# Turning the whole U tiles in an earlier layer, into a DRAM table, and issuing all whole tiles of the expert stage from SP

## The chip, the cores and the metric

The kernel runs on one core of one Trainium2 chip. The metric is the device time of one execution in microseconds (us); 3 executions of the kernel before are shown.

## The reference, cut to what matters

Two transformer blocks follow each other on one sequence of 256 tokens with D = 2048, all in float32. The first is gated linear attention and a SwiGLU feed-forward layer, the second has three attention forms and then a layer of retrieved experts:

```
def swiglu(h, w_gu, w_down):                       # first block; 2 x 5632 columns, then 5632 -> 2048
    g, u = jnp.split(h @ w_gu, 2, axis=-1)
    return (jax.nn.silu(g) * u) @ w_down

def peer_ffn(hn, w_pq, sub_keys, u_tab, v_tab):    # last layer: 16384 experts, 8 heads x top 16 per token
    ...
    expert = ia * PEER_N_KEYS + ib
    gate = jax.nn.softmax(best_s, axis=-1)
    def token_block(args):                         # two blocks of 128 tokens
        a = jnp.einsum('td,ted->te', xb, u_tab[eb])
        hidden = gb.astype(xb.dtype) * jax.nn.gelu(a)
        return jnp.einsum('te,ted->td', hidden, v_tab[eb])
```

Every token thus needs 128 rows of `u_tab` and 128 rows of `v_tab`, each 8 KB, named by indices that are known only once the keys have been scored.

## The kernel before, in words

**Streamed part.** 292 weight tiles of 1 MB pass in order through a ring of 4 slots (`ring`), loaded from SP's queue (L594 is that loop). ACT writes the leading part of each half tile ("unit") to `WH` (L512, or L514 and L515), DVE the rest to `WL` (L527, or L531), and TensorE multiplies leading and rest parts (L633). `WH` and `WL` hold 4 units, so the splitting is at most 4 units ahead of TensorE. The feed-forward layer is 22 chunks of 4 tiles (`gu_chunk`) and then 44 tiles of `w_down`; DVE's part of the latter is a loop of 4 rounds of 8 tiles. POOL has no work there; its next step is the bias load at L1377, after `down_added`.

**Expert stage.** When the last streamed tile is split, the memory of the ring, of `WH`, `WL` and of the operands becomes 12 slots of one row tile each (128 x 2048 floats, 1 MB). `ROW_ORDER` is a fixed list of row tiles that all engines walk in order; row tile `n` uses slot `n % 12`, and is loaded only once row tile `n - 12` has been read. It has four kinds:
- `u`, 256 of them, in 16 groups of 16 (a group is one head of one token block): one expert row per token, gathered by POOL (L1405) and multiplied and summed on DVE (L2566). After a group, its 16 `hidden` values per token are made from these sums.
- `v`, 256 of them: gathered by POOL. Some go to TensorE, as a product with a diagonal matrix that ACT makes from `hidden` (L1873, then L1313), the others to DVE (L2570). `LEADS` says how many v tiles are put among the u tiles of each group, all of these for TensorE; the rest follow after group 15, where about one in eight is TensorE's.
- `turned`, 32 of them: whole tiles of 128 consecutive rows of `u_tab`, loaded by POOL (L1400). These 4096 experts are computed for all tokens, and the gathers leave their rows out. TensorE turns a tile in four parts (L1249), ACT copies each part from PSUM to SBUF (L1895), and TensorE multiplies it with the turned activations (L1260). The last two parts are handled only when the walk reaches the next v or turned tile (`finish_u`). `U_TILES` says how many stand in each group.
- `dense`, 32 of them: the whole tiles of `v_tab` that belong to them, loaded by POOL (L1400), multiplied by TensorE (L1300), all after group 15.

POOL issues every load of this stage in the order of the list, each behind a wait for its slot:

```
                elif n >= ROWS:
                    by, count = ROW_DONE[n - ROWS]
                    pool.wait_ge(sem({"dve": "rows_dve", "pe": "rows_pe", "turned": "raw_turned"}[by]), count)
```

## Time and profile before

| | |
|---|---|
| time, median of 3 executions | 3148.67 us (3145.7 to 3165.38) |
| the profiled execution: its own time, its span | 3147.76 us, 3146.0 us |
| busy in the span: TensorE, DVE, ACT, POOL | 2904.2, 2150.8, 1225.1, 974.6 us |
| expert stage, from POOL's first gather to the end | 1801.9 to 3146.0 us |
| bytes moved by DMA | 793.69 MB, of them 475.94 MB from POOL's queue and 313.73 MB from SP's |

"Busy" of TensorE contains modelled ends of pipelined matmuls. The share of time in which the 16 DMA engines were busy, and the bytes per second that they moved, stand by stretch in the rows below. A wait for several semaphores is put down to the one that came last.

### The profile page before, as it was taken

How to read it: one execution, taken by the hardware profiler on the slowest of the kernel's cores; microseconds unless marked ns; L12 is line 12 of the kernel's file. 1: busy time of each engine (PE TensorE's matmuls, PEld its weight loads, DVE VectorE, ACT ScalarE, POOL GpSimd, SP SyncE). 2: the span in 40 equal slices, each digit the busy share in tenths (PEclk: the TensorE clock that was granted, in tenths of full speed). 3: DMA queues.
4: the chain of work that ended last, by engine and by line, in shares of the span. 5: the costliest groups of instructions: out<-in, count | busy, mean ns of one | idle time of the engine just before them, and what ended most of it. 6: DMA issues, size and time to landing. Idle time of an engine off the chain costs nothing.

```text
span 3146.0 us, 38089 instructions
## 1 busy us (share of the span) xinstructions
PE 2904.2 (92%) x13724; PEld 2187.2 (70%) x13724; DVE 2150.8 (68%) x2908; ACT 1225.1 (39%) x2125; POOL 974.6 (31%) x599
## 2 busy tenths in 40 slices
PE   9999999999999999999999949888888989978987
PEld 8888788888888889998888945554555655533333
DVE  5686665555565545465565887888887668887777
ACT  5555555555553345355655521111111235700000
POOL 0011000000000000000000056777764678886774
PEclk9999999999999999999999979999998999999998
DMA  7444545555555555543443468999997899999997
GB/s 272 146 165 145 185 182 190 188 187 187 188 185 187 187 187 181 189 157 137 153 177 143 182 262 322 366 380 377 370 365 294 321 338 366 360 389 389 387 405 300
DMA packets 128209, 793.69 MB, mean 252 GB/s; under 512 B 30982, under 2 KB 30998, under 8 KB 32670
## 3 DMA queue, kind: packets, MB, share of 16 engines
q0 software_dynamic: 84000, 475.94, 39.2%
q1 hardware_dynamic: 43920, 313.73, 27.4%
q8 instruction: 90, 1.47, 0.2%
q10 hardware_dynamic: 144, 2.10, 0.2%
q14 instruction: 55, 0.45, 0.0%
HBM read 925.55 MB, written 4.22 MB: 296 GB/s over the span
## 4 chain that ended last, share of the span: by engine, by line
PE 69%; POOL 9%; DVE 8%; DMA 8%; issue 3%; ACT 3%; DVEq 0%; ACTq 0%; SPq 0%; POOLq 0%
PE ps L633 48%; POOL rows L1405 9%; PE ps L1313 6%; PE ps L1260 4%; DMA rows<-peer_v 4%; DMA rows<-peer_v,arena 3%; PE ps L1300 3%; DVE arena L2566 3%; PE ps L1249 1%; PE ps L741 1%; DVE WL L531 1%; ACT arena L1885 0%; PE ps L941 0%; PE ps L1291 0%; DMA rows<-peer_u,arena 0%
## 5 line engine op out<-in xcount | busy, mean ns | idle before, releaser
L531 DVE SCALAR_TENSOR_TENSOR WL<-ring,PA,WH 128x512 fp32r<-128x512 f32 x896 | 633.2, 753 | 459.5 <-ACT WH L515 442.6
L1313 PE MATMUL ps<-rows,rstd 128*128 128x512 f32 x1108 | 531.9, 632 | 158.1 <-ACT rstd L1873 103.4
L2566 DVE CUSTOM_DVE_ANT_0 arena<-rows,arena 128x2048 f32<-128x2048 f32 x256 | 586.9, 2292 | 64.5 <-DMA rows<-peer_u,arena 25.8
L514 ACT ACTIVATE WH<-ring,PA 128x512 fp32r<-128x512 f32 x448 | 324.1, 723 | 545.8 <-PE ps L633 398.4
L1405 POOL DMA_INDIRECT rows<-peer_u,arena x256 | 456.2, 1782 | 213.5 <-DVE WL L531 85.1
L1313 PEld LDWEIGHTS ps<-rows,rstd 128*128 128x128 f32 x1108 | 217.8, 202 | 428.6 <-issue 366.6
L1405 POOL DMA_INDIRECT rows<-peer_v,arena x256 | 447.0, 1746 | 171.5 <-issue 65.5
L633 PE MATMUL ps<-WH,HH 128*128 128x512 f32 x1120 | 442.3, 395 | 4.2 <-DVE WL L531 4.2
L633 PE MATMUL ps<-WH,HL 128*128 128x512 f32 x1120 | 437.7, 391 | 0.0
L633 PE MATMUL ps<-WL,HH 128*128 128x512 f32 x1120 | 437.2, 390 | 0.0
L2570 DVE SCALAR_TENSOR_TENSOR XR<-rows,arena,XR 128x2048 f32<-128x2048 f32 (+1 forms) x119 | 276.7, 2325 | 79.9 <-DMA rows<-peer_v,arena 71.3
L515 ACT ACTIVATE WH<-ring,PA 128x512 fp32r<-128x512 f32 x448 | 317.1, 708 | 0.0
L633 PE MATMUL ps<-HH,WH 128*128 128x256 f32 x1088 | 309.5, 284 | 4.7 <-DVE WL L531 3.2
L633 PE MATMUL ps<-HL,WH 128*128 128x256 f32 x1088 | 307.8, 283 | 0.0
L633 PE MATMUL ps<-HH,WL 128*128 128x256 f32 x1088 | 307.8, 283 | 0.0
L1377 POOL DMA_DIRECT2D arena<-bias_rows x2 | 1.8, 908 | 904.0 <-DVE XR L2275 904.0
L1300 PE MATMUL ps<-rows,arena 128*128 128x512 f32 x512 | 236.8, 618 | 37.7 <-DMA rows<-peer_v 37.7
L527 DVE TENSOR_TENSOR WL<-ring,WH 128x1024 fp32r<-128x1024 f32 x128 | 156.0, 1224 | 164.5 <-ACT WH L512 163.8
L633 PEld LDWEIGHTS ps<-WH,HH 128*128 128x128 f32 x1120 | 211.2, 189 | 49.1 <-DVE WL L531 5.7
L633 PEld LDWEIGHTS ps<-WH,HL 128*128 128x128 f32 x1120 | 210.8, 188 | 44.5
L633 PEld LDWEIGHTS ps<-WL,HH 128*128 128x128 f32 x1120 | 211.3, 189 | 43.1 <-issue 0.5
L1300 PEld LDWEIGHTS ps<-rows,arena 128*128 128x128 f32 x512 | 99.7, 198 | 173.0 <-issue 119.2
(391 smaller groups left out, 4186.6 us busy)
## 6 DMA issues: line engine op xcount, KB each, us to landing
ring<-stream SPq DMA_DIRECT2D x292, 1024.0 KB, 4.8
rows<-peer_u POOLq DMA_DIRECT2D x32, 1024.0 KB
rows<-peer_v POOLq DMA_DIRECT2D x32, 1024.0 KB
rows<-peer_u,arena POOLq DMA_INDIRECT x256
rows<-peer_v,arena POOLq DMA_INDIRECT x256
arena<-xT SPq DMA_DIRECT2D x4, 512.0 KB, 8.8
bias_rows<-bias_scratch POOLq DMA_DIRECT2D x1, 2048.0 KB, 11.4
arena<-xT ACTq DMA_DIRECT2D x1, 2048.0 KB, 10.7
```

The lines of the kernel that those rows point to most:

```text
L514: nc.scalar.activation(half_tile(WH, u)[:, 0:CH], raw_half(u)[:, 0:CH], ACT.Copy, scale=gain[0])
L515: nc.scalar.activation(half_tile(WH, u)[:, CH:UNIT], raw_half(u)[:, CH:UNIT], ACT.Copy, scale=gain[1]).then_inc(hi_done, 1)
L527: nc.vector.tensor_tensor(half_tile(WL, u), raw_half(u), half_tile(WH, u).bitcast(f32), ALU.subtract).then_inc(split, 1)
L531: ins = nc.vector.scalar_tensor_tensor(out=half_tile(WL, u)[:, s], in0=raw_half(u)[:, s], scalar=gain[d], in1=half_tile(WH, u).bitcast(f32 ...
L633: last = mm(o, l, r, start=start and n == 0, stop=stop and n == 2)
L741: last = mm(o, k[:, 2 * h + d, tk * P:(tk + 1) * P], q[:, 2 * h + d, tq * P:(tq + 1) * P], start=d == 0, stop=d == 1)
L1260: last = mm(ps[:, 4 + d // 2 % 2, d % 2 * TOK:(d % 2 + 1) * TOK], UT[q % 2][:, k, :], HNT[kt // 8][:, kt % 8, :], start=kt == 0, stop=kt = ...
L1300: last = mm(ps[:, 4 * tt + q, :], DENSE[c][:, tt * P:(tt + 1) * P], rows[:, SLOTS[n % ROWS], q * CH:(q + 1) * CH], start=False, stop=tt == ...
L1313: last = mm(ps[:, 4 * tt + q, :], DIAG[:, k % DIAGS, :], rows[:, SLOTS[n % ROWS], q * CH:(q + 1) * CH], start=n == mine[0], stop=n == ends[q])
L1405: nc.gpsimd.indirect_dma_start(out=rows[:, SLOTS[n % ROWS], :], out_offset=None, in_=u_tab if tab == "u" else v_tab, in_offset=bass.Indire ...
L2566: ins = V.tensor_tensor_reduce(out=JUNK, in0=rows[:, SLOTS[n % ROWS], :], in1=HN[:, tt, :], scale=1.0, scalar=0.0, op0=ALU.mult, op1=ALU.a ...
L2570: ins = V.scalar_tensor_tensor(out=XN[:, tt, s], in0=rows[:, SLOTS[n % ROWS], s], scalar=GA[:, tt, at:at + 1], in1=XN[:, tt, s], op0=ALU.m ...
```

## The change

- The feed-forward layer gets the turning of the 32 U tiles. POOL loads a tile of `u_tab` in four DMAs of 32 rows into two half buffers, in pieces of 512 floats. DVE turns each half with one `transpose` instruction, which turns blocks of 32 x 32 (`turn_tile`, two instructions per tile). POOL stores the 1 MB result to the new DRAM table `u_turned`, waits until it has landed, and loads the next tile. Tiles 0 to 19 are turned in the chunks 1 to 20 of the first matrix, one in each, between its 4th and 5th unit; the other 12 in the `w_down` loop, three in each round of 8 tiles, behind units 1, 6 and 11 of its 16.
- In the expert stage the turned tiles come from `u_turned`, and TensorE multiplies them directly (`turned_rows`). The transposes, ACT's copies and their buffers `UT` are gone. The activations are turned with a stride of 16 elements to match.
- SP issues the 64 whole tiles, POOL only the 512 gathers. Each whole tile still waits for its slot (`slot_free`); the dense ones wait on SP until all 16 groups' `hidden` are made.
- `LEADS` is 8 instead of 5 in groups 8 to 11 and 8 instead of 9 in groups 12 to 14, so 128 instead of 119 v tiles stand among the u tiles, and 128 instead of 137 behind them.

```
-LEADS = [0] + [9] * 7 + [5] * 4 + [9] * 4
+LEADS = [0] + [9] * 7 + [8] * 7 + [9]
 U_TILES = [2] * 8 + [4] * 4 + [0] * 4
...
+        U_TURNED, a = take(a, KD, 4, 32)
+        U_HALF0, _ = take(a, 2, 512)
+        U_HALF = [U_HALF0, rstd[:, :, :].rearrange("p (b x) t -> p b (x t)", b=2)]
+        u_turned = nc.dram_tensor("u_turned", (N_DENSE, P, D), f32, kind="Internal").ap()
...
+            def whole_rows(n, tile):
+                name, landed = ROW_IN[n]
+                slot_free(sp, n)
+                sp.wait_ge(sem(name), landed - 16)
+                sp.dma_start(rows[:, SLOTS[n % ROWS], :], tile).then_inc(sem(name), 16)
...
+            sp.wait_ge(sem("row_in2"), LANDED[2])
+            for n, (tab, d, _) in enumerate(ROW_ORDER):
+                if tab == "turned":
+                    whole_rows(n, u_turned[d])
             sp.wait_ge(sem("hidden"), GROUPS)
             sp.dma_start(GROW, bass.AP(gfin_row.tensor, 0, [[0, P], [1, D]])).then_inc(sem("gfin_in"), 16)
+            for n, (tab, c, _) in enumerate(ROW_ORDER):
+                if tab == "dense":
+                    whole_rows(n, v_tab[c * PEER_KEYS:(c + 1) * PEER_KEYS, :])
...
+            def turned_rows(n, d):
+                pe.wait_ge(sem(ROW_IN[n][0]), ROW_IN[n][1])
+                if d == 0:
+                    pe.wait_ge(sem("norm_leading"), 8 * len(TURNED) + 8)
+                if d % 2 == 0 and d >= 4:
+                    pe.wait_ge(sem("gelu_done"), 1 + d // 2 - 1)
+                u = rows[:, SLOTS[n % ROWS], :].rearrange("p (k i) -> p k i", i=P)
+                for k in range(KD):
+                    last = mm(ps[:, 4 + d // 2 % 2, d % 2 * TOK:(d % 2 + 1) * TOK], u[:, k, :], HNT[k // 8][:, k % 8, :],
+                              start=k == 0, stop=k == KD - 1)
+                last.then_inc(sem("rows_pe"), 1)
...
         @block.gpsimd
...
+            pool.wait_ge(sem("small_weights"), 4)
+            for d in range(N_DENSE + 1):
+                if d:
+                    pool.wait_ge(sem("small_weights"), 4 + 2 * d)
+                    pool.dma_start(u_turned[d - 1], U_TURNED.rearrange("p k b i -> p (k b i)")).then_inc(sem("row_in2"), 16)
+                    pool.wait_ge(sem("row_in2"), 16 * d)
+                if d < N_DENSE:
+                    for b in range(4):
+                        at = (U_ORDER[d] * PEER_KEYS + 32 * b) * D
+                        pool.dma_start(U_HALF[b // 2][:, b % 2, :], bass.AP(u_tab.tensor, at, [[512, 4], [D, 32], [1, 512]])).then_inc(sem(f"row_in{b // 2}"), 16)
...
         @block.vector
...
+            def turn_tile(d, i=0, per=0):
+                for h in range(2):
+                    dve.wait_ge(sem(f"row_in{h}"), i * (32 * per) + 32 * (d + 1))
+                    V.transpose(U_TURNED[:, :, 2 * h:2 * h + 2, :],
+                                U_HALF[h].rearrange("p b (d k) -> p k b d", k=KD)).then_inc(sem("small_weights"), 1)
...
                 for m in range(first, 8):
                     split_lo(dve, 2 * (T_GU + 4 * n) + UNITS + m, i)
+                    if 1 <= n < N_GU - 1 and m == 3:
+                        turn_tile(n - 1, i, 2)
...
+                    for m in range(8):
+                        split_lo(dve, 2 * (T_DOWN + 4 * j) + UNITS + m, i)
+                        if (j, m) in ((0, 1), (0, 6), (1, 3)):
+                            turn_tile(N_GU - 2 + 2 * j + m // 6, i, 3)
```

## Rows read from the trace of the kernel before

**Rows 1.** Page, 40 slices: busy share of the DMA engines in tenths.

```profile
DMA  7444545555555555543443468999997899999997
```

**Rows 2.** Stretches of the expert stage: length, busy and count by engine, clock, DMA share, GB/s.

```profile
core 0: us, PE busy (x) PEld busy (x) DVE busy (x) ACT busy (x) POOL busy (x), PEclk, DMA share, GB/s
1893.00:1967.00 74.00, 66.45 (x224) 39.20 (x223) 57.08 (x115) 11.90 (x30) 54.38 (x35) 0.95 0.91 347
1967.00:2318.00 351.00, 305.88 (x1021) 179.99 (x1020) 305.16 (x547) 53.72 (x135) 273.99 (x160) 0.96 0.97 375
2318.00:2567.50 249.50, 211.32 (x898) 150.60 (x896) 178.72 (x246) 51.54 (x109) 152.43 (x99) 0.96 0.84 315
2567.50:2741.00 173.50, 154.71 (x669) 94.39 (x667) 147.36 (x177) 108.40 (x285) 142.43 (x81) 0.95 0.96 363
2741.00:3134.00 393.00, 339.57 (x803) 149.53 (x802) 309.15 (x159) 21.85 (x50) 275.47 (x177) 0.95 0.96 383
```

**Rows 3.** The same view, two stretches of 8 us late in group 0.

```profile
1880.00:1888.00 8.00, 2.15 (x3) 1.15 (x4) 6.98 (x15) 0.62 (x2) 0.00 (x0) 0.50 0.02 10
1888.00:1896.00 8.00, 8.00 (x31) 5.22 (x31) 6.83 (x6) 0.60 (x1) 0.00 (x0) 0.85 0.00 0
```

**Rows 4.** Timeline, same time: start, duration, instruction, [idle before, releaser].

```profile
1885.85 5.91 PE L1313 MATMUL ps<-rows,rstd 128*128 128x512 f32 x8 [33.28 <-ACT rstd L1873]
...
1896.36 0.99 POOL L1405 DMA_INDIRECT rows<-peer_v,arena  x1 [19.46 <-PE ps L1249]
```

**Rows 5.** Waits, 2318 to 2567: who waited for whom, total us, times, longest.

```profile
POOL rows L1400 <- PE ps L1249: 47.0, 6, 15.7
POOL rows L1405 <- PE ps L1249: 32.4, 10, 6.2
```

**Rows 6.** Timeline of TensorE through one v tile and one turned tile, group 10.

```profile
2378.83 3.67 PE L1313 MATMUL ps<-rows,rstd 128*128 128x512 f32 x8 [1.17 <-ACT rstd L1873]
...
2382.34 1.89 PE L1260 MATMUL ps<-arena,UT 128*128 128x256 f32 x8
...
2384.07 0.60 PE L1249 MATMUL ps<-CO,rows 128*128 128x128 f32 x4
...
2390.13 1.04 PE L1249 MATMUL ps<-CO,rows 128*128 128x128 f32 x8
```

**Rows 7.** Groups of instructions: out<-in, count | busy us, mean ns.

```profile
L1400 POOL DMA_DIRECT2D rows<-peer_u x32 | 18.8, 588 | 57.3 <-PE ps L1249 57.2
```

**Rows 8.** Waits, 2741 to 3134.

```profile
DVE XR L2570 <- DMA rows<-peer_v,arena: 71.3, 39, 4.6
```

**Rows 9.** Stretches of the feed-forward layer: first matrix, then w_down.

```profile
360.00:920.00 560.00, 560.00 (x2535) 462.66 (x2534) 328.38 (x490) 303.55 (x493) 0.00 (x0) 1.00 0.51 186
...
938.00:1182.00 244.00, 243.61 (x1044) 196.19 (x1044) 124.40 (x113) 96.47 (x102) 0.00 (x0) 1.00 0.51 184
```

**Rows 10.** Chain that ended last: start, us; two chunks of the first matrix.

```profile
627.50 21.82 PE ps L633 x96
649.76 21.79 PE ps L633 x96
```

**Rows 11.** Groups of instructions, 938 to 1182: DVE and ACT per unit.

```profile
L527 DVE TENSOR_TENSOR WL<-ring,WH 128x1024 fp32r<-128x1024 f32 x84 | 102.9, 1225 | 117.6 <-ACT WH L512 117.6
...
L2252 DVE TENSOR_SCALAR A_h<-arena 128x1024 fp32r (+1 forms) x9 | 6.2, 689 | 0.0
...
L512 ACT ACTIVATE WH<-ring 128x1024 fp32r<-128x1024 f32 x84 | 89.1, 1061 | 143.2 <-PE ps L633 143.0 <-issue 0.3
```

**Rows 12.** DMA issues: KB each, median us from issue to landing.

```profile
ring<-stream SPq DMA_DIRECT2D x292, 1024.0 KB, 4.8
...
arena<-memT POOLq DMA_DIRECT2D x1, 2048.0 KB, 9.0
arena<-bias_rows POOLq DMA_DIRECT2D x1, 1024.0 KB, 6.9
...
arena<-bias_rows POOLq DMA_DIRECT2D x1, 512.0 KB, 4.9
```

More of the change, by code:

```diff
@@ L94 @@
 ROW_DONE = []
-RAW_TURNED = 24
-_count = {"dve": 0, "pe": 0, "turned": RAW_TURNED}
+_count = {"dve": 0, "pe": 0}
 for _tab, _g, _j in ROW_ORDER:
-    _by = "turned" if _tab == "turned" else "pe" if _tab == "dense" or _tab == "v" and by_matmul(PEER_K * _g + _j - N_LEAD) else "dve"
-    _count[_by] += 4 if _by == "turned" else 1
+    _by = "pe" if _tab in ("dense", "turned") or _tab == "v" and by_matmul(PEER_K * _g + _j - N_LEAD) else "dve"
+    _count[_by] += 1
     ROW_DONE.append((_by, _count[_by]))
-FINISHED_AT = {}
-for _n, (_tab, _g, _j) in enumerate(ROW_ORDER):
-    if _tab == "turned":
-        FINISHED_AT[_g] = next(n for n in range(_n + 1, ROW_LAST) if ROW_ORDER[n][0] in ("v", "turned"))
-SQUARE_AT, POLY_AT, TANH_AT, GELU_AT = ({FINISHED_AT[2 * p + 1] + later: p for p in range(N_DENSE // 2)} for later in (2, 5, 8, 11))
+SQUARE_AT, POLY_AT, TANH_AT, GELU_AT = ({ROW_AT["turned", 2 * p + 1, 0] + later: p for p in range(N_DENSE // 2)} for later in (4, 7, 10, 13))
 BATCH_AT = {}
@@ L118 @@
 FIRST_SHARED = N_ROWS - SHARED
+ROW_IN = []
+_landed = {f"weight_tile_in_slot{_s}": 16 * STREAMED // RING for _s in range(RING)}
+_landed.update({f"row_in{_s}": count for _s, count in enumerate(LANDED)})
+_tiles = 0
+for _n, (_tab, _g, _j) in enumerate(ROW_ORDER):
+    _name = f"row_in{_n % ROWS}"
+    if _tab in ("dense", "turned"):
+        _name, _tiles = f"weight_tile_in_slot{_tiles % RING}", _tiles + 1
+    _landed[_name] += 16
+    ROW_IN.append((_name, _landed[_name]))
 assert LAST_DENSE == N_ROWS - TAIL - 1
@@ L571, in hybrid_block, with slot_free @@
         IN2_AT = [T_IN2 + 4 * n for n in range(5)] + [T_SB + 4 * n for n in range(6)]
+        def slot_free(eng, n):
+            if n < 4:
+                eng.wait_ge(split, 2 * (N_TILES - 3 + n))
+            elif n < ROWS:
+                eng.wait_ge(used, 2 * (N_TILES - (2 if n < 6 else 1 if n < 8 else 0)))
+            else:
+                by, count = ROW_DONE[n - ROWS]
+                eng.wait_ge(sem(f"rows_{by}"), count)
         block = ctx.enter_context(nc.Block())
@@ L1252, in u_products @@
-            def u_products(d, part):
-                q = 4 * d + part
-                if d % 2 == 0 and part == 0 and d >= 4:
-                    pe.wait_ge(sem("gelu_done"), 1 + d // 2 - 1)
-                pe.wait_ge(sem("transposes_kept"), TT + q + 1)
-                for k in range(4):
-                    kt = 4 * part + k
-                    last = mm(ps[:, 4 + d // 2 % 2, d % 2 * TOK:(d % 2 + 1) * TOK], UT[q % 2][:, k, :], HNT[kt // 8][:, kt % 8, :],
-                              start=kt == 0, stop=kt == KD - 1)
-                last.then_inc(used, 1)
@@ L1386, in _ @@
             for n, (tab, g, j) in enumerate(ROW_ORDER):
[L1387 to L1397 removed]
                 if tab in ("dense", "turned"):
[L1399 to L1400 removed]
                     continue
+                slot_free(pool, n)
                 if tab == "u" and j == 0:
@@ L1881, in one_hots @@
                 else:
-                    act.wait_ge(used, 2 * N_TILES + 4 * N_DENSE)
+                    act.wait_ge(sem("rows_pe"), ROW_DONE[ROW_AT["turned", N_DENSE - 1, 0]][1])
                 v = ONE_HOT[n % 2]
@@ L1901, in square_u @@
             def square_u(p):
-                act.wait_ge(used, 2 * N_TILES + 8 * p + 8)
+                act.wait_ge(sem("rows_pe"), ROW_DONE[ROW_AT["turned", 2 * p + 1, 0]][1])
                 if U_ORDER[2 * p] // 8 in (2, 3):
@@ L1942, in _ @@
                     k += 1
-                    if turned is not None:
-                        keep_turned_u(turned, 2)
-                        keep_turned_u(turned, 3)
-                        turned = None
                 if tab == "u" and j == PEER_K - 1:
```

81 lines of the change are left out of this document (14 added, 67 removed).

## The prediction

> **What bounds the kernel now.** I first read the 40 slices of the page. The DMA engines are about half busy up to 1800 us, and 90% or more busy in most of what follows, except in one dip in the middle [rows 1]. So there are two kernels here. In the first TensorE sets the pace: in the feed-forward layer it is busy for 560.00 of 560 us and 243.61 of 244 us, with the DMA engines at 0.51 [rows 9]. The second is the expert stage. I then cut that stage at the first u tile of each group and asked for the busy shares. Groups 2 to 7 (1967 to 2318) have a DMA share of 0.97 at 375 GB/s while TensorE and DVE are each at 0.87; groups 12 to 15 and the v tiles after them are at 0.96 [rows 2]. To check that this is bytes: a gather leaves out a quarter of its rows, so it should move 0.786 MB, and a whole tile 1.049 MB. Six groups of 25 gathers and 2 whole tiles are 130 MB, and 130 MB in 351 us is 372 GB/s, which is the row. After group 15 it is also DVE that waits for data, 71.3 us in all [rows 8].
>
> Where the DMA engines aren't full, TensorE holds a slot. Groups 8 to 11 run at 0.84 and 315 GB/s [rows 2], and there POOL stands 47.0 + 32.4 = 79 us behind TensorE's transposes [rows 5]. The timeline of one turned tile says why: two of its four parts are turned only after the next v tile, each between products (2382.34 to 2390.13 for 16 products that busy TensorE 4 x 1.89 us at most) [rows 6], and the slot is free only then. The worst case is in group 0, where no v tile follows for long: the DMA engines move 10 and then 0 GB/s between 1880 and 1896 [rows 3], POOL waits 19.46 us for a transpose, and TensorE had waited 33.28 us for the first diagonal, made from the first `hidden` [rows 4].
>
> **The change, part by part.** The sum is made against the profiled execution (3147.76 us), which is 0.9 us under the median of the runs shown.
>
> *Group 0.* The turned tiles are now freed as soon as TensorE has multiplied them. POOL can go on by six row tiles, until it meets the slot of the first v tile, which still waits for `hidden`. Five gathers and a whole tile are 5.0 MB, 13 us at 375 GB/s, and the 16 empty us cap it. DVE, which works for 13.8 of those 16 us and isn't helped, may eat some: I take 12 us saved, bounds 0 and 16.
>
> *Groups 8 to 11.* They have 16 u, 8 v and 4 whole tiles now: 24 x 0.786 + 4 x 1.049 = 23.1 MB each, 92.3 MB in four. At groups 2 to 7's 375 GB/s that is 246 us where it took 249.5 [rows 2], though 12 more v tiles are carried. TensorE: a v tile is 3.51 us (2378.83 to 2382.34), 16 products at most 4 x 1.89 = 7.6 us [rows 6], so a group is at most 8 x 3.51 + 4 x 7.6 = 58.5 us under 61.5 of DMA; close, so I take 248 us, 1.5 saved. Bounds: 246, and 269, half way to the 293 us that 92.3 MB take at today's 315 GB/s, if two resources so close get in each other's way. HBM Reference in the Trainium skill (section Access) gives about 358 GB/s as the effective rate of one core when its neighbour streams too, and more alone; with 358 the four groups would take 258 us and the sum would be 10 us less. The 375 and 383 measured here decide.
>
> *Groups 12 to 14.* One gather less each: 3 x 0.786 MB at 363 GB/s [rows 2], 6.5 us saved.
>
> *After group 15.* 128 instead of 137 v tiles: 9 x 0.786 = 7.1 MB at 383 GB/s [rows 2], 18.5 us saved. TensorE's and DVE's shares (0.86 and 0.79) leave the bytes as the bound.
>
> *POOL and SP.* POOL loses 64 issues of 0.588 us [rows 7] and gets them out of its order; with the DMA engines full that frees nothing by itself. SP's queue was empty in this stage; each tile it issues is behind the slot wait of the one before, in the same order as the list. The dense loads wait on SP for the last `hidden`, and the 1 MB gain row goes ahead of them. The first dense tile is ten v tiles behind group 15, and TensorE cannot multiply it before `hidden` and the gates anyway. Two queues side by side move the same bytes. I put all this at 0, bounds 10 us saved (the engines at the 0.97 of groups 2 to 7 throughout, and sooner landings) and 12 us lost (the late first dense tiles hold their slots for some 5 gathers).
>
> *ACT and TensorE.* 128 copies and 512 transposes go; ACT is busy for 51.54 of 249.5 us there [rows 2]. The activations' transposes read with a stride; 32 of them ahead of the first turned tile, 0 to 5 us, not on the u tiles' path: 0.
>
> *Feed-forward layer, DVE's work.* 64 transposes of 128 x 1024. No row has one. The nearest of that size are 0.689 us (one input) and 1.225 us (two inputs) [rows 11]; I take 1.2, and keep 2.4 as the far end, for the strided read. 64 x 1.2 = 77 us lie beside TensorE, on a DVE busy for 124 of 244 us. A unit takes 244 / 88 = 2.77 us; four are buffered; ACT (1.06) and DVE (1.23) need 2.6 with their handovers [rows 11], so DVE can be 3 x 2.77 - 2.6 = 5.7 us late before TensorE waits. A turn of 2.4 us fits, one of 4.8 just so. Price 0.
>
> *Feed-forward layer, the DMAs.* A chain runs from one turn to the next: store issued (0.6), landed, four loads issued (4 x 0.6 and gaps, 2.7 to the last), landed, second half turned (1.2). POOL's own loads beside the stream landed after 9.0 us for 2 MB, 6.9 for 1 MB and 4.9 for 0.5 MB [rows 12], so 1 MB costs about 6.5 and the four loads about 7, if a store costs what a load does. The chain is 0.6 + 6.5 + 7 + 1.2 = 15.3 us. In the first matrix the turns are 649.76 - 627.50 = 22.3 us apart [rows 10], so it hides. In the `w_down` loop three turns share 8 tiles, 44.4 us, 14.8 each. I am 0.5 us over, 12 times, less the 3.4 us of lateness that is left behind a turn: 3 us, and with some slowing of both by each other (the stream's 184 GB/s plus 3 x 2.1 MB in 44.4 us is 326 GB/s, under 375) I take 5 lost. Bounds: 0 (4.8 for 1 MB, the ring's landing [rows 12], gives 0.6 + 4.8 + 5 + 1.2, under 14.8) and 60 (chain of 20 us). ACT's wait for the last store comes about 12 tiles later and hides.
>
> Sum: -12 - 1.5 - 6.5 - 18.5 + 5 = -33.5 us, so 3114, and against the median 3115; rounded up a little for jitter, **3116 us**.
>
> **The rivals.**
>
> *The chain of the turn is the bound in the `w_down` loop* (ends on the slower side). DVE waits in front of its splits, so TensorE waits for every us by which the chain exceeds 14.8, 12 times, less 3.4. The other terms save 38.5 us: from 18.3 us on they are used up, and from 20.9 us on (12 x 6.1 - 3.4 = 70) the kernel is over 1% slower. For it: both transfers share the engines with the stream, the pieces are 2 KB, and no row has such a store. Against: the landings of [rows 12] were beside the same stream. A chain of 23 us costs 95 us: 3205 us. Chance of slower by this, 11%; of one of some 17.6 us that eats most of the gain (3140), 8%.
>
> *The quarter loads run on few DMA engines.* Full, the 16 engines moved 375 to 383 GB/s, 24 GB/s each. On four engines that the stream already fills to half, 1 MB takes 10.9 / 0.49 = 22 us, the chain 0.6 + 6.5 + 25 + 1.2 = 33 us, 11 us over in each of 20 chunks and 18 in each of 12 turns: some 440 us, 3550 us. All DMAs in the rows have 128 rows outermost, so nothing here shows it. DMA: Bandwidth & Descriptors in the Trainium skill (Why a DMA increments its semaphore by 16 and not by 1) says that the number of engines divides the slowest dimension of both sides, which is 4 here, and that POOL's transfers then take engines in turn. By that each load would have its own four and the 7 us would stand. Chance that they don't spread, 4%.
>
> *The expert stage doesn't fill.* Eight v and four turned tiles make groups 8 to 11 TensorE's (58.5 of 61.5 us by my own count), and a v tile whose data is late holds its slot as the turned one did. Groups 8 to 11 take 269 us and the start saves nothing: 3147 instead of 3116. With half of it, 3132. Against: nothing of ACT's stands between the products any more. Chance 17%.
>
> *More than summed.* Groups 2 to 11 have no coupling to the transposes and run at 383 GB/s: 2% of 600 us, 12 us more, and the queue split gives 8: 3096. Chance 13%.
>
> *The code doesn't do what it says:* the same row tiles, the same slots and waits in the same order are there; I see none of it, 1%.
>
> **How the numbers follow.** The forecast has 44%, its own range being 3103 to 3133. 1% is 31 us, about what this kernel's measurement can tell from no change, so faster means under 3117. The forecast gives 28% to faster and 16% to the same; the fuller stage 13% to faster; the unfilled one 14% to the same and 3% to faster; the chain 8% to the same and 11% to slower; the few engines 4% to slower; undone code 1% to the same; 2% are left for the far ends, half on either side. Faster 45, same 39, slower 16. To hold 8 in 10 the range goes from 3094 (the fuller stage) to 3160 (a chain of about 19 us).
>
> **What would show it.** The time of L1313 and L1300 stands; L1249 and L1895 are gone. Right: no empty DMA stretch in group 0; groups 8 to 11 at a DMA share over 0.93; POOL waits for slots only; the last stretch is some 18 us shorter; the w_down stretch is 244 to 250 us with transposes of about 1.2 us. Wrong: TensorE idle before L633 in the w_down loop, released by DVE, and DVE there by a DMA of `u_tab`; or TensorE at 0.95 in groups 8 to 11 with the DMA share still at 0.85.

## The result, and the profile after

The changed kernel takes 3203.94 us (median of 4 runs, 3198.76 to 3206.55), beside 3149.43 us for the kernel before (4 runs). The ratio is 1.0166, interval 1.0132 to 1.0199: 1.7% slower. Forecast were 3116 us and a range of 3094 to 3160. What came is the first rival, the chain of the turn (11%, 3205 us). That its price is met to 1 us is luck: it stands for 95 us lost less 38.5 gained, and 112 and 58 came.

I cut the trace of each kernel's profiled execution at POOL's first gather, which only moves when something ahead of it moves. It stood at 1801.90 us and stands at 1914.10: **112.2 us lost ahead of the expert stage**. From there to the end it was 1344.1 us and is 1286.5: **57.6 us gained in the stage**, where the prediction summed 38.5. So the expert half was right in direction and undersized, and the feed-forward half is wrong by 107 us.

**Ahead of the stage.** A stretch of the first matrix and one of the `w_down` loop, as in [rows 9], in the kernel after (length; busy time and count of TensorE, its weight loads, DVE, ACT, POOL; granted clock; DMA share; GB/s):

```profile
480.00:940.00 460.00, 447.53 (x1987) 366.54 (x1986) 325.16 (x420) 236.19 (x377) 66.03 (x100) 0.99 0.93 270
960.00:1240.00 280.00, 215.89 (x810) 169.25 (x809) 137.90 (x108) 71.91 (x68) 36.75 (x56) 0.84 0.76 210
```

TensorE was all but full in both before [rows 9]. Now it is idle for 12 of 460 us in the first matrix and for 64 of 280 us in the `w_down` loop. Look at the DMA share too. In the first matrix it went from 0.51 to 0.93 (1.8 times), but GB/s only from 186 to 270 (1.45 times). So the engines are busy for longer per byte; I come back to it. Who waits for whom in the `w_down` loop of the kernel after (total us, times, longest):

```profile
POOL u_turned L1382 <- DVE arena L2207: 200.6, 12, 30.6
...
DVE arena L2207 <- DMA arena<-peer_u: 103.4, 11, 13.6
...
PE ps L668 <- DVE WL L538: 64.1, 11, 9.3
...
POOL arena L1387 <- DMA u_turned<-arena: 47.9, 11, 4.7
...
DVE arena L2207 <- DMA rstd<-peer_u: 5.5, 2, 3.6
```

This is what the prediction had named as the sign of its being wrong: TensorE idle behind DVE's split (L633 is L668 now), DVE behind a load of `u_tab` (shown as `peer_u`), 11 times each for about 12 turns. One turn of the loop, POOL first and DVE below (start, duration, instruction, idle before and releaser):

```profile
1012.10 0.59 POOL L1382 DMA_DIRECT2D u_turned<-arena  x1 [17.17 <-DVE arena L2207]
1016.84 1.37 POOL L1387 DMA_DIRECT2D arena<-peer_u  x2 [4.15 <-DMA u_turned<-arena]
1018.19 1.35 POOL L1387 DMA_DIRECT2D rstd<-peer_u  x2
1037.38 0.58 POOL L1382 DMA_DIRECT2D u_turned<-arena  x1 [17.84 <-DVE arena L2207]
```

```profile
1008.13 1.90 DVE L2207 STREAM_TRANSPOSE arena<-arena 128x1024 f32<-128x1024 f32 x1 [13.59 <-DMA arena<-peer_u]
...
1021.55 1.23 DVE L538 TENSOR_TENSOR WL<-ring,WH 128x1024 fp32r<-128x1024 f32 x1 [1.57 <-ACT WH L523]
1033.42 1.89 DVE L2207 STREAM_TRANSPOSE arena<-arena 128x1024 f32<-128x1024 f32 x1 [10.64 <-DMA arena<-peer_u]
1035.23 1.85 DVE L2207 STREAM_TRANSPOSE arena<-rstd 128x1024 f32<-128x1024 f32 x1
```

The chain can be read off: the store and its landing 4.7 us (1012.10 to 1016.84), the loads 16.6 us until the first half is there (to 1033.42), both transposes 3.7 us, 0.3 to the next store: 25.3 us. Over the loop, eleven turns start between 979.2 and 1217.2 us, so 23.8 us apart where the stream left 14.8. Ten times 9.0 us is 90 us, and from the last product of one matrix to that of the other some 92 were lost. In the first matrix the turns are 23.3 us apart on average where the chunk takes 22.2; over its 19 intervals that is the other 20 us.

What the landings look like in the list of DMA issues (KB each, median us from issue to landing), the answer to [rows 12]:

```profile
ring<-stream SPq DMA_DIRECT2D x292, 1024.0 KB, 5.3
u_turned<-arena POOLq DMA_DIRECT2D x32, 1024.0 KB, 4.4
...
arena<-peer_u POOLq DMA_DIRECT2D x64, 256.0 KB, 8.1
rstd<-peer_u POOLq DMA_DIRECT2D x64, 256.0 KB, 12.3
```

A load of 256 KB takes longer than the ring's 1 MB. And the median of 8.1 hides that DVE waits for the later of two.

TensorE is also slower after such a wait. Its timeline around one of them, and the granted clock (third column from the end) behind it:

```profile
1003.24 0.40 PE L668 MATMUL ps<-WH,A_l 128*128 128x512 f32 x1
1012.96 0.79 PE L668 MATMUL ps<-WH,A_h 128*128 128x512 f32 x1 [9.32 <-DVE WL L538]
1013.55 0.63 PE L668 MATMUL ps<-WL,A_h 128*128 128x512 f32 x1
...
1016.53 0.39 PE L668 MATMUL ps<-WH,A_l 128*128 128x512 f32 x1
```

```profile
1013.00:1016.50 3.50, 3.50 (x8) 2.77 (x9) 3.50 (x4) 0.00 (x0) 0.00 (x0) 0.50 0.92 337
```

After 9.32 us of idleness the products start 0.43 us apart for 3.5 us, then 0.23 us apart as before. The granted clock of 1013.0 to 1016.5 is 0.50, the lower of its two levels (1.2 GHz), and 1.00 behind it. Eight products at 0.2 us more are 1.7 us here; behind all waits of the loop it adds up to 24 us. This is no further loss in the time: DVE waited for the loads in eleven of the twelve turns, so the chain sets the pace, and slow products only take the place of waiting (64 us of waits and these 24 are 88 of the 92).

**In the expert stage.** Here I must mend my own rows: the cuts of [rows 2] lie four u tiles late in each group, because four u tiles at the very start had been overlooked. The totals are not touched by it, but for the comparison I cut both kernels anew, at POOL's first gather of groups 1, 2, 8, 12 and 15. The kernel before:

```profile
1850.00:1935.60 85.60, 47.97 (x160) 29.05 (x160) 71.40 (x130) 9.45 (x24) 45.96 (x27) 0.74 0.68 262
1935.60:2285.90 350.30, 306.82 (x999) 177.90 (x1000) 302.95 (x545) 52.24 (x135) 277.58 (x163) 0.96 0.97 372
2285.90:2536.30 250.40, 211.00 (x884) 148.79 (x883) 184.83 (x279) 49.61 (x105) 152.30 (x100) 0.95 0.87 327
2536.30:2704.90 168.60, 148.00 (x631) 92.12 (x630) 138.10 (x163) 96.27 (x246) 132.84 (x76) 0.97 0.94 354
2704.90:3146.00 441.10, 373.27 (x958) 171.14 (x956) 346.64 (x204) 44.45 (x110) 306.40 (x194) 0.94 0.94 372
```

The kernel after, the same places of the list:

```profile
1962.00:2035.70 73.70, 38.04 (x108) 21.23 (x108) 68.43 (x128) 4.72 (x15) 45.41 (x26) 0.75 0.83 303
2035.70:2377.70 342.00, 290.66 (x795) 157.22 (x794) 305.17 (x547) 29.41 (x88) 272.32 (x150) 0.93 0.97 381
2377.70:2615.90 238.20, 222.78 (x745) 143.05 (x744) 184.67 (x279) 21.25 (x58) 169.27 (x96) 0.97 0.96 381
2615.90:2776.40 160.50, 138.09 (x575) 85.27 (x573) 135.43 (x161) 89.40 (x232) 135.89 (x72) 0.95 0.95 358
2776.40:3200.00 423.60, 363.95 (x948) 168.44 (x947) 330.17 (x198) 44.75 (x111) 289.12 (x153) 0.94 0.94 371
```

Row by row that is 11.9 us gained where group 0's stall was, 8.3 in groups 2 to 7, 12.2 in groups 8 to 11, 8.1 in groups 12 to 14, and 17 behind them. Groups 8 to 11 went from a DMA share of 0.87 to 0.96 although they carry 12 more v tiles: TensorE is busy for 223 of 238 us there, and POOL stands behind it for 25.2 us (10 waits), where it stood for 79 us before; at a share of 0.96 little of that can still cost time.

### The profile page after: what moved, and what is told of

It reads as the page before. It is cut to its first block, busy times and chain, and to the rows that moved or that the text cites. A ratio compares the mean times of both kernels' runs of the same rounds, so it can differ in the third digit from the quotient of the medians.

```text
span 3200.6 us, 37235 instructions
## 1 busy us (share of the span) xinstructions
PE 2910.2 (91%) x13276; PEld 2167.9 (68%) x13276; DVE 2241.6 (70%) x2964; ACT 1159.9 (36%) x2005; POOL 1076.5 (34%) x695
## 2 busy tenths in 40 slices
DMA packets 167629, 860.94 MB, mean 269 GB/s; under 512 B 58118, under 2 KB 58134, under 8 KB 67998
## 4 chain that ended last, share of the span: by engine, by line
PE 27%; POOL 12%; DMA 8%; DVE 7%; issue 3%; ACT 2%; DVEq 0%; ACTq 0%; POOLq 0%
PE ps L668 15%; POOL rows L1408 12%; DMA rows<-peer_v,arena 5%; PE ps L1325 5%; DMA rows<-peer_u,arena 3%; PE ps L1282 3%; DVE arena L2562 2%; PE ps L1312 2%; DVE XR L2566 1%; PE ps L976 0%; DVE WL L542 0%; DVE arena L235 0%; DVE arena L228 0%; PE ps L1032 0%; ACT arena L1889 0%
## 5 line engine op out<-in xcount | busy, mean ns | idle before, releaser
L1325 PE MATMUL ps<-rows,rstd 128*128 128x512 f32 x1172 | 577.2, 646 | 172.2 <-DMA rows<-peer_v,arena 89.0
L1325 PEld LDWEIGHTS ps<-rows,rstd 128*128 128x128 f32 x1172 | 236.1, 207 | 481.4 <-issue 355.1
L1408 POOL DMA_INDIRECT rows<-peer_v,arena x256 | 486.1, 1899 | 144.5 <-issue 68.0
L668 PE MATMUL ps<-WH,HH 128*128 128x512 f32 x1120 | 444.8, 397 | 16.8 <-DVE WL L542 16.6
L668 PE MATMUL ps<-WH,HL 128*128 128x512 f32 x1120 | 438.8, 392 | 0.0
L668 PE MATMUL ps<-WL,HH 128*128 128x512 f32 x1120 | 438.4, 391 | 0.0
L668 PE MATMUL ps<-HH,WH 128*128 128x256 f32 x1088 | 310.7, 286 | 6.0 <-DVE WL L542 3.4
L2566 DVE SCALAR_TENSOR_TENSOR XR<-rows,arena,XR 128x2048 f32<-128x2048 f32 (+1 forms) x111 | 257.8, 2322 | 80.0 <-DMA rows<-peer_v,arena 73.0
L668 PE MATMUL ps<-HL,WH 128*128 128x256 f32 x1088 | 308.9, 284 | 0.0
L668 PE MATMUL ps<-HH,WL 128*128 128x256 f32 x1088 | 308.9, 284 | 0.0
L668 PEld LDWEIGHTS ps<-WH,HH 128*128 128x128 f32 x1120 | 211.9, 189 | 65.9 <-DVE WL L542 21.4
L668 PEld LDWEIGHTS ps<-WH,HL 128*128 128x128 f32 x1120 | 211.5, 189 | 45.1
L668 PEld LDWEIGHTS ps<-WL,HH 128*128 128x128 f32 x1120 | 211.9, 189 | 42.9 <-issue 0.5
L523 ACT ACTIVATE WH<-ring 128x1024 fp32r<-128x1024 f32 x128 | 134.6, 1058 | 267.3 <-PE ps L668 260.3
L1282 PE MATMUL ps<-arena,rows 128*128 128x256 f32 x1024 | 226.1, 379 | 1.2 <-ACT arena L1865 1.2
L1282 PEld LDWEIGHTS ps<-arena,rows 128*128 128x128 f32 x1024 | 194.5, 190 | 40.8 <-issue 15.9
## 6 DMA issues: line engine op xcount, KB each, us to landing
rstd<-peer_u POOLq DMA_DIRECT2D x64, 256.0 KB, 12.3
```

Source lines behind the costliest of these rows:

```text
L523: nc.scalar.activation(half_tile(WH, u), raw_half(u), ACT.Copy).then_inc(hi_done, 1)
L668: last = mm(o, l, r, start=start and n == 0, stop=stop and n == 2)
L1282: last = mm(ps[:, 4 + d // 2 % 2, d % 2 * TOK:(d % 2 + 1) * TOK], u[:, k, :], HNT[k // 8][:, k % 8, :], start=k == 0, stop=k == KD - 1)
L1325: last = mm(ps[:, 4 * tt + q, :], DIAG[:, k % DIAGS, :], rows[:, SLOTS[n % ROWS], q * CH:(q + 1) * CH], start=n == mine[0], stop=n == ends[q])
L1408: nc.gpsimd.indirect_dma_start(out=rows[:, SLOTS[n % ROWS], :], out_offset=None, in_=u_tab if tab == "u" else v_tab, in_offset=bass.Indire ...
L2566: ins = V.scalar_tensor_tensor(out=XN[:, tt, s], in0=rows[:, SLOTS[n % ROWS], s], scalar=GA[:, tt, at:at + 1], in1=XN[:, tt, s], op0=ALU.m ...
```

## The experiments

The theories. **Loads' shape**: each of the four loads reads `[[512, 4], [D, 32], [1, 512]]`, so its outermost dimension is the 4 column quarters of its 32 rows, and such loads are slow; DVE's transposes and the bytes are harmless. **DVE's work**: the transposes themselves (1.9 us each) make the splitting late. **Few engines**: each load runs on few of the 16 DMA engines. **Serial chain**: the wait for the store is what makes the chain too long. And for the gain: the coupling to TensorE's transposes, `LEADS`, or SP's queue. The kernel before was timed again beside the experiments (medians 3155.8 to 3159.7 us, 6 to 10 us over that of the result), so ratios compare better than times. "First gather" and "stage" are read as above, from one trace each; the stage of the eleven kernels that share the new expert half takes 1279.8 to 1290.2 us, which shows how far such a figure carries.

| run | time, us (range) | ratio [95%] | first gather | stage |
|---|---|---|---|---|
| changed kernel | 3203.94 (3198.76–3206.55) | 1.0166 [1.0132, 1.0199] | 1914.1 | 1286.5 |
| no_turning | 3094.78 (3093.78–3096.02) | 0.980 [0.9783, 0.9816] | 1809.7 | 1283.7 |
| dve_only | 3090.31 (3087.56–3100.64) | 0.9792 [0.9766, 0.9818] | 1810.0 | 1279.8 |
| rows_outermost | 3115.09 (3110.97–3120.34) | 0.9865 [0.9844, 0.9886] | 1825.6 | 1288.2 |
| pieces_4k | 3101.16 (3095.66–3108.48) | 0.9814 [0.9794, 0.9835] | 1821.8 | 1284.9 |
| rows_of_32 | 3141.03 (3138.27–3142.87) | 0.9956 [0.994, 0.9973] | 1853.1 | 1285.3 |
| early_loads | 3261.84 (3251.0–3268.64) | 1.0329 [1.03, 1.0357] | 1977.9 | 1288.2 |
| two_early | 3205.96 (3203.97–3216.93) | 1.0174 [1.0152, 1.0195] | 1916.1 | 1286.0 |
| two_early_32 | 3089.97 (3083.26–3090.54) | 0.9788 [0.9771, 0.9804] | 1806.9 | 1281.8 |
| two_32 | 3090.32 (3087.55–3093.75) | 0.9787 [0.9747, 0.9826] | 1803.3 | 1282.9 |
| two_per_round | 3161.98 (3152.99–3182.15) | 1.002 [0.9995, 1.0045] | 1871.7 | 1290.2 |
| leads_alone | 3172.31 (3164.26–3181.76) | 1.0058 [1.0034, 1.0083] | 1803.5 | 1360.3 |
| pool_issues | 3100.06 (3093.89–3103.29) | 0.9812 [0.9771, 0.9853] | 1808.5 | 1289.5 |

### Is it the turning, and which part of it?

**no_turning**: no loads, transposes or stores; SP loads the whole U tiles as they stand in the table, so 4096 experts are computed from unturned tiles.

```
-            for d in range(N_DENSE + 1):      # POOL: wait, store, wait, four loads
-                ...
-                    if 1 <= n < N_GU - 1 and m == 3:
-                        turn_tile(n - 1, i, 2)
...
-                        if (j, m) in ((0, 1), (0, 6), (1, 3)):
-                            turn_tile(N_GU - 2 + 2 * j + m // 6, i, 3)
...
-                    whole_rows(n, u_turned[d])
+                    whole_rows(n, u_tab[U_ORDER[d] * PEER_KEYS:(U_ORDER[d] + 1) * PEER_KEYS, :])
```

> The changed kernel without any turning: no loads, no transposes, no stores in the feed-forward layer; the whole U tiles of the expert stage are read from u_tab as they are, so these 4096 experts are computed from unturned tiles. This is the expert half alone. All theories: the first unit of the last part of the kernel comes at the time of before. Theory A (the halves are independent, the expert stage gained 57 us): 3148 - 57 = 3091 us, ratio to before 0.982. Rival (the stage's gain comes partly from its later start or from the table's place in DRAM): 3100 us or more.

**dve_only**: the same, but DVE makes all 64 transposes, of one tile that was loaded once.

```
                 for h in range(2):
-                    dve.wait_ge(sem(f"row_in{h}"), i * (32 * per) + 32 * (d + 1))
+                    dve.wait_ge(sem(f"row_in{h}"), 32)
```

> The changed kernel with all 64 transposes on DVE at their places, but with one tile loaded once, no further loads and no stores; expert stage as in the run without turning. Theory A (the chain of store, loads and transposes is what costs 112 us): the transposes fit into the slack of the splits, within 5 us of the run without turning, about 3093 us; w_down stretch 244 to 250 us. Rival B (DVE's 64 x 1.95 us are themselves too much: 3.8 us in one piece against a lateness of 5.7 us less what the clock takes): 20 us or more over it, 3115 us, with TensorE waiting for DVE in the w_down loop.

Without the turning the first gather is back at 1809.7 us, and the stage keeps its 1284: the two halves of the change are independent, and the loss lies in the turning. (The 8 us over the 1801.9 of before have no cause that a run shows; beside these runs the kernel before was itself 10 us slower than beside the result.) With all of DVE's transposes, but one loaded tile and no stores, nothing of the loss appears: 3090 us. The rows of dve_only for 930 to 1180 us, its stretch and its transposes:

```profile
930.00:1180.00 250.00, 248.10 (x1059) 199.47 (x1058) 168.00 (x135) 95.92 (x95) 0.00 (x0) 0.99 0.52 185
```

```profile
L2200 DVE STREAM_TRANSPOSE arena<-arena 128x1024 f32<-128x1024 f32 x12 | 23.8, 1984 | 0.0
L2200 DVE STREAM_TRANSPOSE arena<-rstd 128x1024 f32<-128x1024 f32 x12 | 23.1, 1922 | 0.0
```

DVE is busy for 168.00 us where the kernel before has 126.58 in the same stretch, and TensorE is as full as there (248.10 of 250 us in both). DVE's work is ruled out; the DMAs remain.

### Which property of the DMAs?

**rows_outermost**: four loads of the same bytes in the same 2 KB pieces, but each over all 128 rows with a quarter of the columns, so that 128 is the outermost dimension. The pieces land in other places, so other values are turned.

```
-                        at = (U_ORDER[d] * PEER_KEYS + 32 * b) * D
-                        pool.dma_start(..., bass.AP(u_tab.tensor, at, [[512, 4], [D, 32], [1, 512]]))...
+                        at = U_ORDER[d] * PEER_KEYS * D + 512 * b
+                        pool.dma_start(..., bass.AP(u_tab.tensor, at, [[D, P], [1, 512]]))...
```

> The changed kernel, but each of the four loads of a tile takes 128 rows of 512 floats with the 128 rows outermost, not 4 groups of 32 rows (what is turned are then other values). Same bytes, same pieces of 2 KB, same number of DMAs. Theory P (the 2 KB pieces cost the engines twice the time per byte): no change against the changed kernel, 3203 us within 8, packets of 4 KB still at some 345 ns. Rival E (a load with 4 outermost runs on few engines, and the four collide): the loads land in 8 us or less instead of 15, the chain goes from 24 to 17 us, 3203 - 70 = 3133 us.

**pieces_4k**: two loads of 128 rows in pieces of 4 KB, so it has half the loads as well.

```
-                    for b in range(4):
-                        ...
+                    for h in range(2):
+                        at = U_ORDER[d] * PEER_KEYS * D + 1024 * h
+                        pool.dma_start(..., bass.AP(u_tab.tensor, at, [[D, P], [1, 1024]]))...
```

> The changed kernel, but a tile is loaded by two DMAs of 128 rows of 1024 floats, 4 KB pieces (other values turned). Theory P (piece size): a 4 KB piece moves at nearly the rate of 8 KB, the load takes 5 us of engine time less and two issues less, the chain 24 to 17 us, 12 x 7 + some 15 of the first matrix saved, 3110 to 3130 us. Rival E (engines) agrees only if the run with rows outermost is fast too. Rival L (latency behind the stream's queue, not pieces): 3 us less per turn, 3165 us.

Same bytes, same pieces, same number of DMAs, another outermost dimension: 89 us come back. The `w_down` stretch of rows_outermost and its landings:

```profile
930.00:1180.00 250.00, 232.84 (x969) 183.82 (x968) 157.72 (x126) 86.51 (x84) 29.95 (x56) 0.98 0.73 265
```

```profile
u_turned<-arena POOLq DMA_DIRECT2D x32, 1024.0 KB, 4.4
arena<-peer_u POOLq DMA_DIRECT2D x64, 256.0 KB, 4.1
rstd<-peer_u POOLq DMA_DIRECT2D x64, 256.0 KB, 6.6
```

The store is unchanged at 4.4 us; the loads land in half the time (4.1 and 6.6 instead of 8.1 and 12.3). The turns of this kernel are 22.2 us apart in the first matrix, so they cost nothing there, and 17.1 in `w_down`, still more than 14.8: some 16 us are lost against a first gather at 1810. The size of the pieces is a small thing beside it (pieces_4k, ratio 0.9814 against 0.9865).

How the loads come to be twice as slow shows in the single packets of the trace. For POOL's queue, packets of 4096 bytes (two pieces of 2 KB), first matrix (480 to 940 us), with the number of engines that are at work on them while any is, and the time from a tile's first packet to its last:

| kernel | outermost | mean ns of a packet | engines at work at once, mean | first to last packet, us |
|---|---|---|---|---|
| changed kernel | 4 | 343 | 8.5 | 10.9 |
| rows_outermost | 128 | 190 | 9.0 | 5.8 |
| pieces_4k | 128 | 181 | 11.0 | 4.2 |
| rows_of_32, below | 32 | 271 | 8.6 | 8.9 |
| early_loads, below | 4 | 276 | 5.1 | 15.1 |

The mean number of engines is nearly the same in the first two rows, but a packet takes 1.8 times as long: that is the DMA share that had grown by more than the bytes. The mean hides one thing. In the first 3 us behind a tile's first packet only 4 to 6 engines on average work on the loads in the changed kernel, where rows_outermost has 13 to 16 from 0.5 to 2 us; the others are busy with the stream. So in the first matrix the loads also begin on few engines. In the `w_down` loop, where most of the loss is, that ends early: 14 to 16 engines from 1.5 us on, packets of 376 ns against 196, and 9.4 us from first to last against 5.1. There the slow packet is the difference. How the two share the loss in the first matrix, no run separates. The loads with 4 outermost also bring packets of 8 bytes, 768 per tile, that no other shape has: 24,576 packets under 512 bytes more than in rows_outermost (58118 and 33542), which is 32 x 768. They are short (11 ns each), so the count of them is a mark, not the time itself. Why the packet is slow is not shown.

### The shape in a kernel that still turns right, and the order of store and loads

**rows_of_32**: eight loads of 32 partitions each, 32 outermost; the same places are filled.

```
+                    for h in range(2):
+                        for q in range(4):
+                            at = (U_ORDER[d] * PEER_KEYS + 64 * h) * D + 512 * q
+                            pool.dma_start(U_HALF[h][32 * q:32 * q + 32, :, :],
+                                           bass.AP(u_tab.tensor, at, [[D, 32], [32 * D, 2], [1, 512]]))...
```

> The changed kernel, with the same pieces of 2 KB to the same places, but in eight loads of 32 rows x 2 x 512 floats with the 32 rows outermost instead of four with 4 groups outermost; computes the reference. Theory E (the outermost 4 makes each packet take 343 ns instead of 159 ns): packets near 190 ns, DMA share of the first matrix 0.77 instead of 0.93, chain some 18 us because eight issues take 5.4 us, about 3120 us. Rival W (the cost lies in writing only 32 neighbouring partitions at a time, or in 128 KB transfers): packets stay over 300 ns, 3190 us or more.

**early_loads**: the next tile's loads are issued right behind the store, not once it has landed; DVE waits for the store instead, before it overwrites the result.

```
                     pool.dma_start(u_turned[d - 1], ...).then_inc(sem("row_in2"), 16)
-                    pool.wait_ge(sem("row_in2"), 16 * d)
                 if d < N_DENSE:
                     ...                                   # the four loads
+                if d:
+                    pool.wait_ge(sem("row_in2"), 16 * d)
+                    pool.sem_inc(sem("u_stored"), 1)
```

> The changed kernel, but POOL issues the next tile's loads right behind the store, without waiting for it to land; DVE waits for the landed store before it turns the next tile. Computes the reference. If the chain is what costs, taking the store's 4.7 us out of it saves 12 x 4.7 in w_down and the lateness of the first matrix, some 60 to 70 us: 3135 to 3145 us. Rival (the DMA engines are full, the order of the chain doesn't matter): within 15 us of the changed kernel.

**two_early**: early_loads with a looser timetable: 21 turns in the first matrix, 2 in each round of `w_down`, 3 behind it.

```
-                        if (j, m) in ((0, 1), (0, 6), (1, 3)):
-                            turn_tile(N_GU - 2 + 2 * j + m // 6, i, 3)
+                        if m == 2:
+                            turn_tile(N_GU - 1 + j, i, 2)
...
+            W.units_to(base + 2)
+            turn_tile(N_GU + 7)
```

> As the run with early loads, with 21 turns in the first matrix, two in each of the four rounds of 8 tiles of w_down (22 us apart) and three behind them. Computes the reference. Chain theory: the chain of 20 us fits into 22, so the feed-forward layer costs at most 10 us over before: 3095 to 3105 us. Rival (full engines, slow packets, cost the stream's landings too): 3120 us or more.

rows_of_32 has the first matrix full again (TensorE 450.00 of 450 us from 480 us on) and 61 us of the 112 back. It came between theory and rival, though: packets of 271 ns where some 190 were expected, a DMA share of 0.87 instead of 0.77, 3141 us instead of 3120. So 32 outermost lies between 4 and 128, and with eight loads of a quarter of the partitions it also differs in more than the outermost dimension. In `w_down` its turns are still 19.8 us apart. The two others missed. I had thought to take the 4.7 us of the store out of the chain, and the kernel got 58 us slower. Two turns of early_loads on POOL, and its landings:

```profile
614.78 0.58 POOL L1382 DMA_DIRECT2D u_turned<-arena  x1 [23.02 <-DVE arena L2210]
615.36 1.36 POOL L1386 DMA_DIRECT2D arena<-peer_u  x2
616.72 1.34 POOL L1386 DMA_DIRECT2D rstd<-peer_u  x2
641.88 0.58 POOL L1382 DMA_DIRECT2D u_turned<-arena  x1 [23.82 <-DVE arena L2210]
```

```profile
u_turned<-arena POOLq DMA_DIRECT2D x32, 1024.0 KB, 5.1
arena<-peer_u POOLq DMA_DIRECT2D x64, 256.0 KB, 9.0
rstd<-peer_u POOLq DMA_DIRECT2D x64, 256.0 KB, 18.9
```

The chain is 27.1 us in this turn: the second half's loads land 18.9 us after their issue (median) instead of 12.3. Issued beside the store, the loads' packets are each no slower (276 ns), but fewer run at a time, 5.1 engines on average, and 1 to 4 for 56% of their time. So it is few engines at once that stretches them here, and the wait for the store, which looked like pure cost, was worth more than it took. What the store has to do with it is not shown. The looser timetable of two_early gives 62 us of it back (first gather 1916 instead of 1978), which leaves it where the changed kernel was.

**two_early_32**: two_early with the eight loads of rows_of_32. **two_32**: the same, but the loads wait for the store as in the changed kernel. **two_per_round**: the looser timetable alone, with the changed kernel's four loads.

> The run with two turns per round and early loads, with the eight loads of 32 rows. Computes the reference. Chain theory with E: no wait of TensorE is left, 3091 to 3097 us, as the run without turning; the step from the run before shows what the slow packets still cost when the chain fits.

> Two turns per round with 32 rows outermost, but the loads wait for the store to land, as in the changed kernel. Computes the reference. A chain of 4.7 + 13.5 + 3.8 = 22 us against 22.2 between turns: fits, 3090 to 3096 us. Rival (early loads are needed): 3105 us or more.

> The changed kernel with two turns per round of w_down instead of three, one more in the first matrix and three behind the rounds; loads with 4 outermost and behind the store, as in the changed kernel. Computes the reference. Chain of 24 us against 22.2: some 2 us over per turn, 12 turns, and the first matrix's 19: first gather at 1840 us, 3130 us. Rival (as in the run with early loads, slow packets starve TensorE wherever the turns stand): 3180 us or more.

With 32 outermost and two turns a round everything is hidden: first gathers at 1803 and 1807, the place of the kernel before. The `w_down` stretch of two_32:

```profile
930.00:1180.00 250.00, 248.10 (x1066) 199.47 (x1065) 167.12 (x138) 97.00 (x100) 53.74 (x100) 1.00 0.85 283
```

TensorE's 248.10 us are those of the kernel before, while the DMA engines move 283 GB/s instead of 185. Whether the loads wait for the store is worth nothing once they are of this shape (3089.97 and 3090.32 us). And the timetable alone doesn't do it: two_per_round leaves the slow loads where they are, and its first gather is at 1872, 42 us of the 112 back. Its waits for 930 to 1180 us:

```profile
DVE arena L2207 <- DMA arena<-peer_u: 52.7, 9, 9.0
...
PE ps L668 <- DVE WL L538: 27.3, 9, 4.9
```

I had expected 3130 of it, from a chain of 24 us, and it took 3162: the eight turns of its `w_down` loop are 26.9 us apart on average (23.9 to 30.6), where the stream leaves them 22.4. Both versions with 32 rows and two turns beat the kernel before (by 2.1%) and the changed one (by 3.7%, as 0.9787 to 1.0166).

### Where the stage's gain comes from

**leads_alone**: the kernel before with only the new list.

```
-LEADS = [0] + [9] * 7 + [5] * 4 + [9] * 4
+LEADS = [0] + [9] * 7 + [8] * 7 + [9]
```

> The kernel before with nothing but LEADS of the changed one (9 more v tiles among the u tiles), tiles still turned in the expert stage. Computes the reference. Theory S (the stage was held by the transposes' slots in groups 8 to 11, so more v tiles there need the transposes gone): no gain, the stage takes 1340 to 1350 us as before's 1344.1. Rival (the moved v tiles alone, which fill DMA time that lay idle, are the gain): 18 us or more off the stage, 1325 us.

**pool_issues**: two_early_32 with POOL issuing all 64 whole tiles in list order and SP none.

```
+                if tab in ("dense", "turned"):
+                    ...
+                    pool.dma_start(rows[:, SLOTS[n % ROWS], :], tile).then_inc(sem(name), 16)
```

> The fastest kernel so far (two turns per round, early loads, 32 rows outermost), with POOL issuing the 64 whole tiles in the order of the list, SP none. Computes the reference. As predicted (the queue is worth 0, bounds 10 saved and 12 lost): its stage takes 1282 us within 6. Rival (a second queue is part of the 57 us): 1292 us or more.

The list alone makes the stage 16 us longer. Groups 8 to 11 of leads_alone, and who waits for TensorE there:

```profile
2287.40:2574.10 286.70, 247.06 (x976) 164.48 (x975) 184.40 (x279) 54.49 (x119) 170.11 (x113) 0.98 0.84 318
```

```profile
POOL rows L1405 <- PE ps L1249: 91.6, 14, 19.4
```

Those groups take 36 us more than before; 4 us come back in groups 12 to 14 and 16 behind them. Their 92.3 MB ran at 318 GB/s, where fewer bytes had run at 327 before; only without TensorE's transposes do they reach 381. So the new `LEADS` costs 16 us alone and goes well with the turned table (286.7 to 238.2 us for the same tiles). No run has the turned table with the old list, so what the list adds to the gain is not shown.

SP's queue shows in groups 2 to 7. In pool_issues:

```profile
1930.40:2279.40 349.00, 286.20 (x808) 156.43 (x807) 305.84 (x547) 29.09 (x88) 275.21 (x163) 0.95 0.96 373
```

349.0 us at 373 GB/s, as in the kernel before, where POOL issued too (350.3 at 372). The eleven kernels in which SP issues the whole tiles took 340.2 to 344.4 us, so 5 to 9 us there are the queue's. For the whole stage no gain is shown: 1289.5 us lie within the 1279.8 to 1290.2 us of those eleven, for groups 8 to 11 are a little shorter in pool_issues (234.5 against 235.8 to 241.9 us). The times (3100.06 and 3089.97 us) are 10 us apart, with ratios whose intervals overlap.

## Why the prediction was wrong

*What bounds the kernel before.* Right: TensorE in the feed-forward layer, bytes in the stage, TensorE's slots in groups 0 and 8 to 11. Once the slots are decoupled the DMA share is 0.96, and leads_alone shows that more v tiles without that cost 36 us.

*Group 0, 12 us.* Right: 11.9 in the stretch that had the stall. The wait of 19.46 us for a transpose is gone. A shorter gap is left, and it is DVE's, which the prediction had named as what may eat some of the gain:

```profile
1980.00:1988.00 8.00, 0.00 (x0) 0.00 (x0) 7.38 (x10) 0.00 (x0) 4.28 (x2) 0.50 0.21 59
```

```profile
1983.41 3.04 POOL L1408 DMA_INDIRECT rows<-peer_u,arena  x1 [8.68 <-DVE arena L2562]
```

*Groups 8 to 11, 1.5 us.* Right in kind, undersized: 12.2. I took 375 GB/s and then rounded up for TensorE; they run at 381 on the new cuts. The 269 us of the far bound didn't come. The prediction had weighed another rate, the 358 GB/s of HBM Reference in the Trainium skill; it stands in the section Specifications (TRN2), not under Access, and it is what the page gives a core whose neighbour streams too. The trace of this one core has 381 over groups 2 to 11.

*Groups 12 to 14, and after group 15: 6.5 and 18.5.* Right: 8.1 and 17.

*POOL and SP, 0 with a bound of 10 saved.* 5 to 9 us in groups 2 to 7; over the stage not told from 0.

*DVE's transposes.* 1.95 us instead of 1.2, inside the bounds, and free as predicted where the data are there: dve_only turns for 3.9 us at a time, and TensorE stays full.

**The feed-forward layer's DMAs, 5 us: the step that failed; 112 us were lost.** Of its chain, 0.6 + 6.5 + 7 + 1.2 = 15.3 us, each term against what was measured: the store lands after 4.4 us, not 6.5, so that term was too high. DVE's end is 3.7, for both halves follow each other once both are late: 2.5 too low. The four loads were put at 7 us, "if a store costs what a load does" and if a load costs what POOL's other loads do; they took 16.6. In that turn of 25.3 us the terms are +9.6 for the loads, +2.5 for DVE, -2.4 for the store with its issue and +0.3 for the handover, 10.0 in all: the error is the loads. The rows that I scaled from [rows 12] had 128 rows outermost, as I wrote myself under the second rival, and the only thing that I asked of the shape was on how many engines it runs. With 128 outermost the chain is 17.1 us (rows_outermost), which would have been the small rival of 17.6 us; with 4 it is 23.8 on average. My far bound, a chain of 20 us and 60 us lost, was too near: nothing in the rows excluded a load twice as slow. Why this shape costs twice as much stays open.

*The rivals.* The chain came by its mechanism, and its length was well placed: priced for 23 us, measured 23.8. The 3205 us beside 3203.94 are luck all the same: the rival lost 95 us where 112 were lost, and kept a gain of 38.5 where 57.6 came. Its formula (12 times the excess over 14.8, less 3.4) gives 105 us for 23.8; measured were 92 in `w_down` plus 20 in the first matrix, which I had thought safe at 22.3 us. TensorE's half clock (24 us in all) wasn't counted and needn't be, since the turns set the pace. The few engines: as priced, 1 MB on four engines and 3550 us, this didn't come, and in the `w_down` loop up to 16 engines work on the loads. But the rival wasn't empty: the first 3 us of the loads in the first matrix ran on 4 to 6 engines, and early_loads had 5.1 at once. DMA: Bandwidth & Descriptors in the Trainium skill (Why a DMA increments its semaphore by 16 and not by 1) has each such load take four engines, in turn. The trace is in keeping with it, with a median of 4 at work 0.5 us behind a tile's first packet and up to 16 later; its packets don't name their engine, so it isn't shown. What the prediction left out was the time of the single packet. The stage that doesn't fill: excluded. More than summed: this was the true case for the stage alone, 57.6 us.

## What to carry to other kernels

A landing time belongs to a shape, not to a number of bytes: before a DMA's time is taken from a row of the same size, compare the outermost dimension of both, and where no row has it, keep more than twice the time as a bound (7 us were summed here and 16.6 came). When a chain of DMAs must fit between two events of a stream, write down the room in both places (14.8 and 22.3 us here) and ask which term, doubled, breaks it. And compare DMA share with GB/s: when the share rises faster, each byte holds an engine for longer. Here the new timetable alone gave back 42 us of 112, the new shape alone 61 (32 outermost) or 89 (128), and timetable and shape of 32 together all of it.

## What was unexpected of the hardware

- Loads over 4 x 32 rows took 343 ns per 4 KB packet and brought 768 packets of 8 bytes per 1 MB tile; with 128 outermost 181 to 190 ns, with 32 outermost 258 to 271 ns, and none of the small ones (first matrix).
- The same slow loads landed later still when issued right behind a store on their queue (18.9 instead of 12.3 us), though each packet was shorter (276 instead of 343 ns). The 32-row ones went from 7.0 to 9.2 us, at the same kernel time.
- A store of 1 MB from POOL landed after 4.4 us beside the stream, sooner than the stream's own loads (5.3).
- A `transpose` of 128 x 1024 floats with a strided read took 1.87 to 1.98 us on DVE (means), against 1.22 for a two-input instruction of that size.
- With 64 of 576 loads issued from SP's queue instead of POOL's, a stretch that was already at a DMA share of 0.96 took 340.2 to 344.4 us instead of 349.0; the stretch behind it did not gain.
